# A decoder block on one core: seven unused 104x104 products a column added around the inversion's last level

## What is computed

```
S_t = S_{t-1} diag(w_t) + (S_{t-1} (-kk_t)) (kk_t * a_t)^T + v_t k_t^T
y_t = S_t r_t
```

## Time and profile before

| what | value |
| --- | --- |
| median of three runs | 2846.53 us (2842.26, 2846.53, 2847.11) |
| the profiled execution's own time | 2845.26 us |
| its span, first to last instruction | 2843.7 us |
| PE busy | 2676.1 us, 94% |
| DVE busy | 1899.6 us, 67% |
| ACT busy | 1322.5 us, 47% |
| mean granted clock of PE | 0.975 |

### The profile page before, as it was taken

The page is one execution under the profiler, slowest core; times in us unless marked ns, Lnnn a source line. Parts: engine busy times, 40 slices in busy tenths (PEclk is TensorE's granted clock), DMA queues, the critical chain, the costliest instruction groups (busy, mean ns, idle before and its releaser), DMA issues.

```text
span 2843.7 us, 55480 instructions
## 1 busy us (share of the span) xinstructions
PE 2676.1 (94%) x21067; PEld 2274.2 (80%) x21067; DVE 1899.6 (67%) x2197; ACT 1322.5 (47%) x1436; POOL 526.5 (19%) x537
## 2 busy tenths in 40 slices
PE   7899999999898999897899999999999999999995
PEld 5787878788898999775677777778788888888884
DVE  8676848485422111344667667677599999999997
ACT  3313131221221111243555566565577777777776
POOL 5100101010000000123232332322311222222221
PEclk9999999999999999998899999999999999999998
DMA  4000000000111112331687686776799999999999
GB/s 120 16 2 17 9 9 16 10 16 2 30 44 52 32 42 67 97 103 57 261 285 259 252 285 255 261 273 252 269 397 381 381 380 381 380 380 381 381 380 341
DMA packets 143095, 537.09 MB, mean 189 GB/s; under 512 B 17842, under 2 KB 71448, under 8 KB 89478
## 3 DMA queue, kind: packets, MB, share of 16 engines
q1 hardware_dynamic: 122438, 492.78, 46.2%
q0 software_dynamic: 20544, 42.74, 6.0%
HBM read 501.04 MB, written 34.42 MB: 188 GB/s over the span
## 4 chain that ended last, share of the span: by engine, by line
PE 84%; DVE 6%; DMA 4%; issue 3%; ACT 2%; POOL 0%; SPq 0%; DVEq 0%; ACTq 0%; POOLq 0%
PE bank L891 33%; PE bank L2113 12%; PE bank L2115 12%; PE bank L2114 12%; PE bank L2122 4%; DMA raw_first<-in_w_e_down 2%; PE bank L2091 2%; PE bank L2023 1%; PE bank L2025 1%; PE bank L2024 1%; DVE xmix L655 1%; PE bank L2149 1%; DVE nrm L795 1%; PE bank L2101 1%; PE bank L2128 1%
## 5 line engine op out<-in xcount | busy, mean ns | idle before, releaser
L1936 DVE TENSOR_TENSOR w_lo<-raw_first,w_hi 128x2048 fp32r<-128x2048 f32 x275 | 619.2, 2283 | 81.7 <-ACT w_hi L1708 81.0
L1708 ACT ACTIVATE w_hi<-raw_first 128x2048 fp32r<-128x2048 f32 x276 | 531.2, 1925 | 206.7 <-DMA raw_first<-in_w_e_up 58.5
L2113 PE MATMUL bank<-w_hi,x_hi 128*128 128x512 f32 x1088 | 433.9, 399 | 2.3 <-ACT yo_rows L1758 2.3
L2115 PE MATMUL bank<-w_hi,x_lo 128*128 128x512 f32 x1088 | 425.5, 391 | 0.0
L2114 PE MATMUL bank<-w_lo,x_hi 128*128 128x512 f32 x1088 | 424.8, 390 | 0.0
L1936 DVE TENSOR_TENSOR w_lo<-raw_rest,w_hi 128x2048 fp32r<-128x2048 f32 x136 | 308.6, 2284 | 15.8 <-ACT w_hi L1708 15.5
L1708 ACT ACTIVATE w_hi<-raw_rest 128x2048 fp32r<-128x2048 f32 x136 | 260.5, 1918 | 116.6 <-PE bank L2149 42.2
L891 PE MATMUL bank<-xm_hi,ring_hi 128*128 128x260 f32 x896 | 261.9, 292 | 20.0 <-DVE dz L852 8.2
L891 PE MATMUL bank<-xm_lo,ring_hi 128*128 128x260 f32 x896 | 255.1, 285 | 0.0
L891 PE MATMUL bank<-xm_hi,ring_lo 128*128 128x260 f32 x896 | 255.1, 285 | 0.0
L2113 PEld LDWEIGHTS bank<-w_hi,x_hi 128*128 128x128 f32 x1088 | 205.0, 188 | 51.4 <-issue 10.2
(11 more groups left out here) (380 smaller groups left out, 4633.6 us busy)
## 6 DMA issues: line engine op xcount, KB each, us to landing
raw_first<-in_w_e_up SPq DMA_DIRECT2D x138, 1024.0 KB, 6.1
raw_first<-in_w_e_gate SPq DMA_DIRECT2D x70, 1024.0 KB, 6.4
raw_rest<-in_w_e_gate SPq DMA_DIRECT2D x70, 1024.0 KB, 4.8
raw_first<-in_w_e_down SPq DMA_DIRECT2D x68, 1024.0 KB, 7.1
raw_rest<-in_w_e_down SPq DMA_DIRECT2D x68, 1024.0 KB, 8.3
ring<-in_w_in SPq DMA_DIRECT2D x40, 512.0 KB, 3.9
hn_d<-hn SPq DMA_DIRECT2D x10, 416.0 KB
h_d<-h_all SPq DMA_DIRECT2D x10, 416.0 KB
```

Of the source, the lines that this page charges most:

```text
L1708: nc.scalar.activation(w_hi[:, j % NRING, :, :], raw_piece(j), ACT.Copy).then_inc(hi_done, 1)
L1936: nc.vector.tensor_tensor(w_lo[:, j % NRING, :, :], raw_piece(j), w_hi[:, j % NRING, :, :].bitcast(f32), ALU.subtract).then_inc(lo_done, 1)
L2113: nc.tensor.matmul(ps[:, :], hi, w_hi[:, slot, k, :], start=start and k == 0, stop=False)
L2115: ins = nc.tensor.matmul(ps[:, :], lo, w_hi[:, slot, k, :], start=False, stop=stop and k == HK - 1)
```

## The change

A helper `keep_busy(n)` issues n products of AT's slots 0 and 3 of unit 0 (104x104) into bank 1. It is called once after the D products of each step of level 6, twice at the last block, and once more between the end of the loop and the wait for the last R copy. Nothing reads what they write. No mark and no wait is added.

```diff
@@ -983,6 +983,11 @@
                 pe_j.mark(ins, ('X', l, b))
 
+            def keep_busy(n):
+
+                for _ in range(n):
+                    mm(bank[1][0:TP, 0:TP], AT[:, 0, 0, :], AT[:, 0, 3, :])
+
             for i in range(len(STEPS) + 2):
@@ -1010,12 +1015,15 @@
                             ins = mm(bank[4 + (i - 1) % 2][0:TP, TP * m:TP * (m + 1)], P1[:, (i - 1) % 2, m, :], Rm[:, u, :])
                     pe_j.mark(ins, ('D', l, b))
+                    if l == LEVELS - 1:
+                        keep_busy(2 if b == NB - 1 else 1)
                 if i >= 2 and STEPS[i - 2][0] == LEVELS - 2:
...
                 if i in XA_AFTER:
                     state_products(XA_AFTER.index(i))
+            keep_busy(1)
             dve_j.done(pe, ('R', LEVELS - 1, NB - 1), j)
```

## The result

The changed kernel takes **2854.66 us** (median of ten runs, 2852.03 to 2861.79), the kernel before 2846.91 us in its ten: ratio **1.0031, 95% interval 1.0023 to 1.0039**, slower by some 8 us. The forecast was 2841.6 us with a range of 2837.5 to 2848.5. It missed in size and in sign.

The account below looks back on a forecast made before the run. PE was taken to bound the kernel through waits and half-clock stretches. A held clock gives back 7.5 us and added products cost 2.6, so -4.9 us from the median 2846.53: 2841.6 us, range 2837.5 to 2848.5.

Parts of the forecast that it names:

- What bounds the kernel: PE bounds, busy 94% of the span; its clock falls to half at the end of the last level in all columns.
- Price of one and what is hidden: Each added product costs 0.185 us; after idle time is filled, 0.65 us a column, 2.6 us in all, is paid.
- the four step products: After D of blocks 0 to 3: first costs 0.18 us, second mostly absorbed, third half, fourth in the 0.33 us gap.
- The last three: Behind the last D, 0.55 us of products fill PE's 0.41 us wait for DVE's R copy, leaving 0.14 us.
- What it may give: With enough PE work the clock behind the last level does not fall, giving back 7.5 us, between 6.8 and 8.1.
- three signs of being wrong: Clock still falls in two or more columns, last level grows over 1.3 us, or a fall appears at a new place.
- The rule against this change: Only long idle gaps lower PE's clock; gaps here are at most 0.41 us, so filling them only costs 2.6 us.
- it falls anyway: Seven products too few to hold the clock behind the last level; only the 2.6 us cost remains, 2849.1 us; chance 0.14.
- it moves: A column start, the third, begins to lose its clock instead, costing 2.9 us, giving 2844.5 us; chance 0.12.
- Slower: Third and fourth products fully delay the last block's P and D, clock still falling: 2851.7 us and up; chance 0.04.

Follow-up runs that it names:

- e3: Changed kernel with three unused 104x104 products instead of one after the D products of blocks 0 to 3; ratio 1.0020 to the kernel before.
- e7: Changed kernel with two unused 104x104 products instead of one after the D products of blocks 0 to 3; ratio 1.0001 to the kernel before.
- e2: Changed kernel with only the four products after D of blocks 0 to 3, without the three behind the last D; ratio 1.0024 to the kernel before.
- e8: Changed kernel with fifteen small products (64 rows by 40 columns) a column, three a step and three at the end; ratio 0.9994 to the kernel before.
- e1: Changed kernel with only the three products behind the last D, without the four after D of blocks 0 to 3; ratio 1.0004 to the kernel before.
- e10: Changed kernel with eleven small products (64 rows by 40 columns) a column, two a step and three at the end; ratio 0.9987 to the kernel before.

## Why the prediction was wrong

**What bounds the kernel.** Right: PE bounds the stretch, and a fall of its clock behind the last level is paid nearly in full. The price was well read too. I took 7.27 us for the work behind the level at full clock; measured 7.48, so a fall costs 1.5 us in three columns and 2.8 in the first, 7.3 us in all where I had 6.8 to 8.1.

**Price of one and what is hidden.** One product 0.185 us: right (0.18 between e3 and e7). The sum of 0.65 us a column was too low, though inside its bounds of 0.56 and 1.30: at full clock it is 1.10 us, 4.4 in all. The terms that were missed are those of the four step products: I had most of the second absorbed, half of the third, and the fourth wholly covered by the 0.33 us gap. In truth the P behind an added product no longer starts inside the D ahead of it (192.89 and 193.25 in the changed timeline, against the earlier trace rows), so each moves everything behind it by at least its length, and e2 measures 0.86 us for them. The last three had 0.14 and took 0.24.

**What it may give: the step that failed.** I put down 7.5 us for a clock that would no longer fall, and argued that the change "fills just what separates the two" stretches, the busy 3.99 and the less busy 3.2 of 4.00 us. The profile after has 4.00 of 4.00 and the clock falls in four columns of four. The busy share cannot show the difference: a small record counts for 0.22 us while the next of them starts 0.03 to 0.04 us behind it, as in the kernel before, column 0:
```profile
192.15 0.23 PE L891 MATMUL bank<-Rw,P 40*64 40x40 f32 x1
192.18 0.22 PE L891 MATMUL bank<-Tw,AT 64*40 64x64 f32 x1
192.21 0.23 PE L891 MATMUL bank<-Rw,P 40*64 40x40 f32 x1
```
So the step "if PE has enough to do, the clock does not fall" took PE without a gap for PE with enough to do, and that failed: four falls without a gap, and none in e8 with two. The work of level 6 differs from that of level 5 in its size above all (the earlier trace rows had both shapes in them), and that I had read and then not used. All three signs of being wrong that the prediction named are there: the clock falls in four columns, the level grows by 1.53 to 2.12 us, and a fall appears where there was none.

**The rule against this change.** The windows fit neither it nor my reading. The Trainium skill, page "TensorE: Matmul & The Clock Gate", section "HAM oscillation — how this bites in real kernels", explains the clock's fall by long idle gaps. The trace does not bear this out here: the changed kernel has no gap at all where its clock falls. That nothing would be gained and the cost be paid came true nevertheless, for another reason. On the same page of the Trainium skill the section "A second HAM failure mode: psum-queue depth-cycling" has short idles between groups of products bring the clock down, which I took for the better fit. It does not explain this case either: the clock fell with no idle time in 4.00 us, and held in e8 with waits of 0.20 and 0.28 us.

**The rival "it falls anyway"** was the case, to which I gave 0.14. Its price of 2.6 us was wrong twice. The first term is 4.4. The second was missing: the clock came back later, after 6.8 instead of 3.4 us in two more columns, and the last added products themselves ran at half clock. That they prolonged the half-clock stretch, because they prolong the small work in it, is my reading; no run shows it by itself, and e1 and e2 have stretches of both lengths. The sum: full-clock work in the two spans is 4 x (8.32 + 7.48) = 63.2 us of 73.8, so 10.6 us are lost to the clock; before, 4 x (7.22 + 7.48) = 58.8 of 66.1, so 7.3. That is 3.3 us more, and 4.4 + 3.3 = 7.7 us, all of the difference in the table above.

**The rival "it moves"** happened besides in the profiled execution (the start of column 3): the clock of these starts comes and goes from run to run in the experiments as well. Its price of 2.9 us was too high. From the reader of the fifth X copy in column 2 to the first P product of level 6 in column 3, the stretch with that start in it, took 141.35 us in place of 140.47: 0.9 us. **Slower** by over 0.2% had a chance of 0.06, because I had the cost and the lost clock as one or the other. They add up.

## What to carry to other kernels

Work added to keep PE's clock up has to be judged by the clock it leaves, not by the gaps it fills: too little of it cost twice here, its own time and more time lost at half clock. Choose short filler that can run beside the real products (other rows and columns of the array), or take work that has to be done anyway and spread it over the weak stretch. And test two doses: here one product a step lost 0.31%, two a step nothing, and the kernel's own work with small filler gained 0.28%.

## What the runs showed of the hardware that was not expected

- The granted clock fell to 0.50 with PE busy for 4.00 of the 4.00 us before, without a single wait in them; and it held in e10, column 1, with 3.42 of 4.00.
- Products of 64 rows by 40 columns on partitions 0 to 63 were free beside those on 64 to 103 and in the waits between them: seven left the level at 7.21 us, fifteen at 7.40. One over 104 rows in the same place cost 0.215 us, more than its own 0.18.
- The same work with the same busy share kept its clock in one column and lost it in the next (e10), so a single column or profile can mislead, and the falls are better counted over several columns and executions.
